# A two-block mixer and transformer kernel: weight rows stored as even and odd halves, and every weight product reading the two halves in turn

## The chip, the cores and the metric

The kernel runs on one core of one Trainium2 chip. The metric is the time of one execution on the device in microseconds. Three runs of the kernel before are given, and one execution of it was taken with the hardware profiler.

## What is computed

Two layers in a row on 256 tokens of width 2048, all in float32. The first block has an mLSTM and an HGRN2 branch behind one input projection, the second a spatial gating unit, stick-breaking attention and a gated feed-forward part. Both end with a gate on a small second input. Cut to the products with weight matrices, which the change touches:

```
def first_block(x, p, ...):
    proj = rmsnorm(x, norm_w) @ w_in                 # 2048 x 8200
    ...
    h = x + y @ w_out                                # 2048 x 2048
    e = p @ w_pe                                     # 256 x 2048
    h = h + sigmoid(rmsnorm(h, pe_norm_w) @ w_pg) * e
    return rmsnorm(h, final_norm_w)

def second_block(x, p, ...):
    proj = rmsnorm_2(x, attn_norm_g) @ w_in          # 2048 x 9216
    ...
    merged = sigmoid(g_a) * (y_a @ w_up_a) + sigmoid(g_b) * (y_b @ w_up_b)
    x = x + merged @ w_o
    hid = rmsnorm_2(x, ffn_norm_g) @ w_ffn_in        # 2048 x 11264
    x = x + (silu(gate) * up) @ w_ffn_out            # 5632 x 2048
    ple = p @ w_ple
    return x + sigmoid(rmsnorm_2(x, ple_norm_g) @ w_ple_gate) * ple
```

## The kernel before

Tokens lie on the output partitions: a product has 128 tokens as its stationary operand (a 128x128 block of the transposed activations) and a row of 512 weight columns, on 128 partitions, as its moving operand. The 256 tokens are T = 2 such blocks. An output slab is 512 columns (COLS) wide and takes two PSUM banks (`acc2(n)`, one for each token block). A piece is two blocks of 128 weight rows (PK = 2) of one slab, 128 x 2 x 512 numbers.

Float32 products are made of three products in the type float32r. The weights are split into a high part `whi` and a low part `wlo`, the activations into `act[0]` and `act[1]`; high times high, low times high and high times low are added. So a standard piece (the function `piece`, L1342 and L1347) issues 2 blocks x 2 token blocks x 3 = 12 products of 128x512. There are 512 of these pieces. For part of the second block's large matrices a seven-product scheme (M1 to M7) is used in place of eight half-size ones. Its pieces (`s_piece`, L1699 and L1703) treat one block of 128 tokens, or a sum of two, and so issue 6 products each. There are 336 of them. `first_piece` (L1370 to L1381) and `last_piece` (L1358) are the first and the last standard piece with finer waits.

A piece travels so. The SP queue loads weights from DRAM in pairs of pieces into `raw`, a ring of 8 places. ScalarE copies a place to `whi` (L915, for the seven-product scheme L1164), which rounds it to float32r. VectorE writes `wlo` as `raw` minus `whi` (L1851, L2507). Both `whi` and `wlo` are rings of 4 (RING). PE waits for `hi_ready` before the products with `whi` and for `lo_ready` before those with `wlo`, and gives the place back by `piece_used`, for which ScalarE waits before it writes the place again:

```
                act.activation(whi[:, g % RING], raw_piece(g), ACT.Copy).then_inc(hi_ready, 1)
                dve.tensor_tensor(wlo[:, g % RING], raw_piece(g), whi[:, g % RING].bitcast(F32), ALU.subtract)\
                    .then_inc(lo_ready, 1)
```

The weight blocks that the seven-product scheme needs as sums are made element by element, by transfers that add in DRAM (`summed`) and by VectorE.

Between the pieces, at fixed places of PE's program, stand the other matmuls: transposes through the identity, the recurrent branches, attention scores (L1589, L1590, moving `qT`, plain float32) and the spatial mixing (L1627). The last takes as its moving operand `vs[:, :, g * P:(g + 1) * P]`, 2 x 128 columns, that is two runs of 128 neighbours.

The order of the work is written out by hand on each engine, the seven-product part by the class `Plan`. The change alters none of it. The host function `_lay_out` brings the weights into the order in which the transfers read them. Before the change, the 512 columns of a slab lie in each weight row as they come.

In the profile's names of a matmul the output stands left of the arrow, and right of it the moving operand and then the stationary one.

Of the kernel before, what the change touches and what calls it, by code (L numbers as in the profile page):

```python
# [36 lines left out]
P = 128  # L37
# [4 lines left out]
COLS = 512  # L42
PK = 2

RAW = 8
RING = 4
# [265 lines left out]
def two_blocks_kernel(nc, A, out):  # L312
# [4 lines left out]
    with ctx:  # L317
# [20 lines left out]
        whi = sb("whi", [P, RING, PK, COLS], F32R)  # L338
        wlo = sb("wlo", [P, RING, PK, COLS], F32R)
# [9 lines left out]
        actA = [sb(f"actA_{x}", [P, KD, S], F32R, at=ra) for x in ("hi", "lo")]  # L349
# [141 lines left out]
        def aux_taken(eng, u, i=0):  # L491

            eng.wait_ge(aux_free[u % 4], u // 4 + 1 + i)
# [140 lines left out]
        def acc2(n):  # L634
            return acc[:, 2 * (n % 2):2 * (n % 2) + 2, :]
# [673 lines left out]
        def _(pe):  # L1309
# [19 lines left out]
            def free(u):  # L1329
                if u >= 4:  # L1330
                    aux_taken(pe, u - 4)

            def piece(n, p, act, k, last, i=0, slabs=0):

                g = SLABS[n][p]
                if p == 0 and n >= 2:
                    slab_taken(pe, n - 2, i * (slabs // 2))
                pe.wait_ge(hi_ready, g + 1 + i * ROUND)
                for c in range(PK):
                    for t in range(T):  # L1340
                        for x in range(2):
                            pe.matmul(acc2(n)[:, t, :], act[x][:, k + c, t * P:(t + 1) * P], whi[:, g % RING, c, :],  # L1342
                                      start=(p == 0 and c == 0 and x == 0), stop=False)
                pe.wait_ge(lo_ready, g + 1 + i * ROUND)
                for c in range(PK):
                    for t in range(T):
                        ins = pe.matmul(acc2(n)[:, t, :], act[0][:, k + c, t * P:(t + 1) * P], wlo[:, g % RING, c, :],  # L1347
                                        start=False, stop=(last and c == PK - 1))
                ins.then_inc(piece_used, 1)

            def last_piece(n, p, act, k):

                g = SLABS[n][p]
                pe.wait_ge(lo_ready, g + 1)
                for t in range(T):
                    for c in range(PK):
                        for x, w in ((0, whi), (1, whi), (0, wlo)):
                            ins = pe.matmul(acc2(n)[:, t, :], act[x][:, k + c, t * P:(t + 1) * P], w[:, g % RING, c, :],  # L1358
                                            start=False, stop=(c == PK - 1 and w is wlo))
                    ins.then_inc(sem("last_tile"), 1)  # L1360

# [3 lines left out]
            def first_piece():  # L1365

                pe.wait_ge(sem("x_hi"), 1)
                pe.wait_ge(sem("first_half_hi"), 1)
                for t in range(T):
                    pe.matmul(acc2(0)[:, t, :], actA[0][:, 0, t * P:(t + 1) * P], whi[:, 0, 0, :], start=True, stop=False)  # L1370
                pe.wait_ge(sem("x_lo"), 1)
                for t in range(T):
                    pe.matmul(acc2(0)[:, t, :], actA[1][:, 0, t * P:(t + 1) * P], whi[:, 0, 0, :], start=False, stop=False)
                pe.wait_ge(hi_ready, 1)
                for t in range(T):
                    for x in range(2):
                        pe.matmul(acc2(0)[:, t, :], actA[x][:, 1, t * P:(t + 1) * P], whi[:, 0, 1, :], start=False, stop=False)
                pe.wait_ge(lo_ready, 1)
                for c in range(PK):
                    for t in range(T):  # L1380
                        ins = pe.matmul(acc2(0)[:, t, :], actA[0][:, c, t * P:(t + 1) * P], wlo[:, 0, c, :], start=False, stop=False)  # L1381
                ins.then_inc(piece_used, 1)

            def warm(n):
# [115 lines left out]
            for s in range(16):  # L1500
                n = FIRST["A"] + s
                for p in range(8):
                    w = s * 8 + p
# [39 lines left out]
            for s in range(4):  # L1543
                n = FIRST["C"] + s
                for p in range(8):
                    k = (KD // 2 + p * PK) % KD
# [19 lines left out]
            for s in range(4):  # L1566
                n = FIRST["D"] + s
# [63 lines left out]
            for s in range(10):  # L1631
                n = FIRST["E1"] + s
                for p in range(8):
# [3 lines left out]
                    w = s * 8 + p  # L1637
# [21 lines left out]
            def s_piece(g, c, m, q):  # L1659

                if m == "M1" and q == 0:
                    if c == 0:
                        for i in range(4):
                            aux_taken(pe, AUX[("ybT", i)])
                    else:
                        pe.wait_ge(sem("s_second_row"), c)
                    if c == M_GROUPS:
                        for i in range(4, 8):
                            aux_taken(pe, AUX[("hH", i)])
                    if c > M_GROUPS:  # L1670
                        pe.wait_ge(sem("tr_taken"), fills_before(g, "e"))
                if m == "M2" and q == 0 and c > 0:
                    pe.wait_ge(sem("hid_odd_ready"), c)
                    pe.wait_ge(sem("tr_taken"), fills_before(g, "a"))
                if m == "M7" and q == 0:
                    pe.wait_ge(sem("merge_forms_lo" if c < M_GROUPS else "forms_lo"), 4)
                if m == "M5" and q == 0 and c > 0:
                    pe.wait_ge(sem("s_first_row"), c)
                if m == "M6" and q == 0:
                    pe.wait_ge(sem("s_first"), c + 1)  # L1680
                if m == "M3" and q == 0:
                    pe.wait_ge(sem("s_fifth"), c + 1)
                o = s_bank(c, m)
                if m == "M7" and q == 0 and c >= M_GROUPS:
                    pe.wait_ge(sem("tr_taken"), fills_before(g, "d"))
                if m == "M4" and q == 0:
                    pe.wait_ge(sem("s_sixth"), c + 1)
                whole, parts = (actB, merge_form_T) if c < M_GROUPS else (actA, formT)

                def lhs(x, k):  # L1690
                    if m in S_FORM:
                        return parts[x][:, S_FORM[m], k, :]
                    return whole[x][:, KD // 2 + k, P:S] if m == "M4" else whole[x][:, k if m == "M1" else KD // 2 + k, 0:P]

                onto = m in ("M6", "M3")
                pe.wait_ge(hi_ready, g + 1)
                for k in range(PK):
                    for x in range(2):
                        pe.matmul(o, lhs(x, q * PK + k), whi[:, g % RING, k, :], start=(q == 0 and k == 0 and x == 0 and not onto),  # L1699
                                  stop=False, skip_group_check=onto)  # L1700
                pe.wait_ge(lo_ready, g + 1)
                for k in range(PK):
                    ins = pe.matmul(o, lhs(0, q * PK + k), wlo[:, g % RING, k, :], start=False, stop=(q == 3 and k == PK - 1),  # L1703
                                    skip_group_check=onto)
                ins.then_inc(piece_used, 1)

# [7 lines left out]
            for kind, g, *x in PLAN.merge:  # L1714
                if kind == "s":
                    s_piece(g, x[0], x[2], x[3])
                else:
                    n, role, j, q, p = x
# [6 lines left out]
                t = g - PLAN.g_plan  # L1725
# [15 lines left out]
            for s in range(4):  # L1741
                n = FIRST["G"] + s
# [52 lines left out]
            for kind, g, *x in PLAN.ffn:  # L1795
                if kind == "s":
                    s_piece(g, x[0], x[2], x[3])
                else:
                    n, role, j, q, p = x
# [955 lines left out]

def _lay_out(inputs, np):

    def blocks(w):
        k, n = w.shape
        return w.reshape(k // 512, 4, P, n // COLS, COLS).transpose(3, 0, 2, 1, 4)  # L2760

    def short(w):
        return w.reshape(PK, P, w.shape[1] // COLS, COLS).transpose(1, 2, 0, 3)

    laid = {name: inputs[name] for name in _AS_THEY_ARE}
    x = inputs["x"][0]
    laid["x"] = x.reshape(T, P, D).transpose(1, 0, 2)
    columns = x.T.reshape(KD, P, S).transpose(1, 0, 2).reshape(P, KD * S)
    laid["x_gain_and_columns"] = np.concatenate([inputs["norm_w"].reshape(KD, P).T, columns], axis=1)
    for name in _WEIGHTS:  # L2770
        laid[name] = blocks(inputs[name][0])
    w = inputs["w_in"][0]
    laid["w_in"] = blocks(np.concatenate([w[:, :MI], w[:, HQ:]], axis=1))
    laid["w_in_gates"] = w[:, MI:HQ].reshape(KD, P, HQ - MI).transpose(1, 0, 2)
    for name in ("w_pe", "w_ple_2"):
        laid[name] = short(inputs[name][0])
    for name in ("p", "p_2"):
        laid[name] = inputs[name][0, 0].T.reshape(PK, P, S).transpose(1, 0, 2)
    laid["w_s_2"] = inputs["w_s_2"][0].transpose(2, 0, 1)
    laid["vectors"] = np.concatenate([inputs[name].reshape(-1, P) for name in _VECTORS], axis=0).T  # L2780
    return {name: np.ascontiguousarray(a) for name, a in laid.items()}
# [16 lines left out]
```

## Time and profile before

| | before |
|---|---|
| median of 3 runs | 1984.99 us |
| lowest, highest | 1984.66, 1985.69 us |
| profiled execution: span from the first to the last instruction | 1982.4 us |
| PE busy | 1973.1 us (100%) |
| load of stationary operands (PEld) busy | 1642.8 us (83%) |
| VectorE (DVE) busy | 1476.6 us (74%) |
| ScalarE (ACT) busy | 1147.5 us (58%) |
| GpSimd (POOL) busy | 114.5 us (6%) |
| moved by DMA | 535.95 MB, 270 GB/s in the mean |

The page gives no other time for the profiled execution than its span, so the span stands for it here. Busy time is the time in which at least one instruction of the engine was under way. Matmuls overlap, and the end of one is modelled, so the pace of PE is read from the starts of the instructions and not from their lengths. The granted clock is the share of full speed that TensorE's clock had.

### The profile page before, as it was taken

The page shows a single profiled execution, that of the slowest core. Times are in us where ns is not written, and L with a number is a line of the kernel's source. Part 1 is how long each engine was busy: PE and PEld are TensorE (multiplying, and loading weights), DVE is VectorE, ACT ScalarE, POOL GpSimd, SP SyncE. Part 2 cuts the span into 40 slices and gives each one's busy share as a digit, 9 for nine tenths or more (in the row PEclk, how much of TensorE's full clock was granted, in tenths as well). Part 3 has the DMA queues.
Part 4 walks back from the last instruction along what each step waited for, and adds up shares of the span by engine and source line. Part 5 has one row for each costly group of instructions (what it writes and reads, how often), then busy time and mean ns, then how long its engine had stood idle before and what let it go on. Part 6 is the DMA issues. An engine that isn't in the chain of part 4 may idle for free.

```text
span 1982.4 us, 23547 instructions
## 1 busy us (share of the span) xinstructions
PE 1973.1 (100%) x9126; PEld 1642.8 (83%) x9126; DVE 1476.6 (74%) x1571; ACT 1147.5 (58%) x1417; POOL 114.5 (6%) x140
## 2 busy tenths in 40 slices
PE   9999999999999999999999999999999999999999
PEld 7888888888888888888888888888888888888887
DVE  6877776555666666768888657888988898888764
ACT  7546444554466455556666445666666666666553
POOL 1000010000001110000000000000000000000000
PEclk9999999999999999999999999999999999999999
DMA  9788798999889999858797876788878887877553
GB/s 377 255 250 278 234 322 275 323 327 313 278 287 298 342 341 299 255 195 253 283 299 244 313 242 238 236 299 278 273 229 303 271 264 240 308 251 235 209 178 125
DMA packets 86816, 535.95 MB, mean 270 GB/s; under 512 B 10417, under 2 KB 11185, under 8 KB 40753
## 3 DMA queue, kind: packets, MB, share of 16 engines
q1 hardware_dynamic: 72736, 458.69, 60.9%
q0 software_dynamic: 13824, 75.50, 20.0%
q8 instruction: 72, 1.18, 0.2%
q10 hardware_dynamic: 144, 0.26, 0.0%
q14 instruction: 40, 0.32, 0.0%
HBM read 529.69 MB, written 105.38 MB: 320 GB/s over the span
## 4 chain that ended last, share of the span: by engine, by line
PE 96%; DVE 2%; DMA 1%; ACT 1%; issue 0%; SPq 0%; DVEq 0%; ACTq 0%
PE acc L1342 45%; PE acc L1347 22%; PE aux L1699 15%; PE aux L1703 8%; PE aux L1325 1%; PE aux L1415 1%; DMA raw<-in_w_in 1%; DVE wlo L1851 1%; PE aux L1780 0%; DVE wlo L2507 0%; ACT whi L915 0%; PE aux L1405 0%; PE aux L1430 0%; DVE att_z L2353 0%; PE aux L1316 0%
## 5 line engine op out<-in xcount | busy, mean ns | idle before, releaser
L1851 DVE TENSOR_TENSOR wlo<-raw,whi 128x1024 fp32r<-128x1024 f32 x512 | 624.2, 1225 | 359.7 <-ACT whi L915 350.2
L915 ACT ACTIVATE whi<-raw 128x1024 fp32r<-128x1024 f32 x511 | 537.3, 1058 | 535.0 <-PE acc L1347 490.0
L1342 PE MATMUL acc<-whi,actA_hi 128*128 128x512 f32 x892 | 351.6, 394 | 0.0
L1342 PE MATMUL acc<-whi,actA_lo 128*128 128x512 f32 x892 | 347.4, 390 | 0.0
L1342 PE MATMUL acc<-whi,actB_hi 128*128 128x512 f32 x796 | 312.7, 393 | 0.2 <-DVE actB_lo L2624 0.2
L1342 PE MATMUL acc<-whi,actB_lo 128*128 128x512 f32 x796 | 309.9, 389 | 0.0
L1164 ACT ACTIVATE whi<-ple 128x1024 fp32r<-128x1024 f32 x192 | 202.3, 1060 | 136.0 <-PE acc L1347 87.4
L2507 DVE TENSOR_TENSOR wlo<-ple,whi 128x1024 fp32r<-128x1024 f32 x192 | 231.9, 1223 | 37.6 <-ACT whi L1164 30.6
L1347 PE MATMUL acc<-wlo,actA_hi 128*128 128x512 f32 x892 | 238.7, 389 | 0.0
L1347 PE MATMUL acc<-wlo,actB_hi 128*128 128x512 f32 x796 | 213.2, 390 | 1.2 <-DVE wlo L1851 1.2
L2507 DVE TENSOR_TENSOR wlo<-raw,whi 128x1024 fp32r<-128x1024 f32 x144 | 175.4, 1223 | 36.1 <-ACT whi L1164 30.9
L1347 PEld LDWEIGHTS acc<-wlo,actA_hi 128*128 128x128 f32 x892 | 167.5, 188 | 35.1
L1342 PEld LDWEIGHTS acc<-whi,actA_hi 128*128 128x128 f32 x892 | 167.6, 188 | 34.2 <-issue 0.3
L1164 ACT ACTIVATE whi<-raw 128x1024 fp32r<-128x1024 f32 x144 | 152.6, 1060 | 73.9 <-PE acc L1347 48.9
L1342 PEld LDWEIGHTS acc<-whi,actA_lo 128*128 128x128 f32 x892 | 167.6, 188 | 33.5
L1347 PEld LDWEIGHTS acc<-wlo,actB_hi 128*128 128x128 f32 x796 | 149.3, 188 | 33.0 <-DVE wlo L1851 2.0
L1342 PEld LDWEIGHTS acc<-whi,actB_hi 128*128 128x128 f32 x796 | 149.5, 188 | 31.0 <-DVE actB_lo L2624 0.9
L1342 PEld LDWEIGHTS acc<-whi,actB_lo 128*128 128x128 f32 x796 | 149.6, 188 | 30.1
L1699 PE MATMUL aux<-whi,actB_hi 128*128 128x512 f32 x360 | 140.4, 390 | 0.0
L1699 PE MATMUL aux<-whi,actB_lo 128*128 128x512 f32 x360 | 140.1, 389 | 0.0
L1703 PE MATMUL aux<-wlo,actB_hi 128*128 128x512 f32 x360 | 111.0, 389 | 0.3 <-DVE wlo L2507 0.3
L1699 PE MATMUL aux<-whi,actA_hi 128*128 128x512 f32 x216 | 85.1, 394 | 0.0
(360 smaller groups left out, 2391.9 us busy)
## 6 DMA issues: line engine op xcount, KB each, us to landing
raw<-in_w_in SPq DMA_DIRECT2D x108, 1024.0 KB, 7.6
raw<-in_w_ffn_out SPq DMA_DIRECT2D x44, 1024.0 KB, 7.0
summed<-in_w_ffn_in POOLq DMA_DIRECT2D x36, 1024.0 KB, 11.9
raw<-in_w_ffn_in SPq DMA_DIRECT2D x72, 512.0 KB, 7.5
ple<-summed SPq DMA_DIRECT2D x24, 1024.0 KB, 4.8
raw<-summed SPq DMA_DIRECT2D x48, 512.0 KB, 4.8
ple<-in_w_ffn_in SPq DMA_DIRECT2D x18, 1024.0 KB, 7.6
ple<-in_w_ffn_in POOLq DMA_DIRECT2D x36, 512.0 KB, 9.8
```

Of the source, the lines that this page charges most:

```text
L915: act.activation(whi[:, g % RING], raw_piece(g), ACT.Copy).then_inc(hi_ready, 1)
L1164: act.activation(whi[:, g % RING], s_source(c, m, q), ACT.Copy).then_inc(hi_ready, 1)
L1325: ins = pe.transpose(bank(u)[:, c * S + t * P:c * S + (t + 1) * P], src[:, t, (c0 + c) * P:(c0 + c + 1) * P], ident[:, :])
L1342: pe.matmul(acc2(n)[:, t, :], act[x][:, k + c, t * P:(t + 1) * P], whi[:, g % RING, c, :], start=(p == 0 and c == 0 and x == 0), stop=False)
L1347: ins = pe.matmul(acc2(n)[:, t, :], act[0][:, k + c, t * P:(t + 1) * P], wlo[:, g % RING, c, :], start=False, stop=(last and c == PK - 1))
L1415: ins = pe.matmul(bank(u)[:, j * m:(j + 1) * m], Kp[n % 2][:, c:c + P], Qp[n % 2][:, j * m:(j + 1) * m], start=True, stop=True)
L1699: pe.matmul(o, lhs(x, q * PK + k), whi[:, g % RING, k, :], start=(q == 0 and k == 0 and x == 0 and not onto), stop=False, skip_group_check ...
L1703: ins = pe.matmul(o, lhs(0, q * PK + k), wlo[:, g % RING, k, :], start=False, stop=(q == 3 and k == PK - 1), skip_group_check=onto)
L1851: dve.tensor_tensor(wlo[:, g % RING], raw_piece(g), whi[:, g % RING].bitcast(F32), ALU.subtract)\
L2507: dve.tensor_tensor(wlo[:, g % RING], s_source(c, m, q), whi[:, g % RING].bitcast(F32), ALU.subtract)\
```

## The change

On the host, in each row of 512 columns of every weight matrix the even columns come first and then the odd ones (`woven` in `_lay_out`). `w_in_gates`, the 8 gate columns, and the small arrays stay as they are. On PE, the moving operand of every weight product is no longer the row of 512 as it lies, but a pattern of 256 x 2 elements over it: element 0 of the first half, element 0 of the second half, element 1 of the first half, and so on (`woven` beside `piece`). So column j of the output is again column j of the weights. The pattern's inner step is 256 elements (1024 bytes), its outer step one element.

All products keep their shape, number and order; every engine's and every queue's instructions stand in the order of before. Buffers, waits and the stationary operands are unchanged.

```
+            def woven(ring, g, c):
+                return ring[:, g % RING, c, :].rearrange("p (h j) -> p j h", h=2)
...
             def piece(n, p, act, k, last, i=0, slabs=0):
...
-                            pe.matmul(acc2(n)[:, t, :], act[x][:, k + c, t * P:(t + 1) * P], whi[:, g % RING, c, :],
+                            pe.matmul(acc2(n)[:, t, :], act[x][:, k + c, t * P:(t + 1) * P], woven(whi, g, c),
...
-                        ins = pe.matmul(acc2(n)[:, t, :], act[0][:, k + c, t * P:(t + 1) * P], wlo[:, g % RING, c, :],
+                        ins = pe.matmul(acc2(n)[:, t, :], act[0][:, k + c, t * P:(t + 1) * P], woven(wlo, g, c),
...
-                        pe.matmul(o, lhs(x, q * PK + k), whi[:, g % RING, k, :], start=(q == 0 and k == 0 and x == 0 and not onto),
+                        pe.matmul(o, lhs(x, q * PK + k), woven(whi, g, k), start=(q == 0 and k == 0 and x == 0 and not onto),
...
-                    ins = pe.matmul(o, lhs(0, q * PK + k), wlo[:, g % RING, k, :], start=False, stop=(q == 3 and k == PK - 1),
+                    ins = pe.matmul(o, lhs(0, q * PK + k), woven(wlo, g, k), start=False, stop=(q == 3 and k == PK - 1),
...
 def _lay_out(inputs, np):
+    def woven(w):
+        k, n = w.shape
+        return w.reshape(k, n // COLS, COLS // 2, 2).swapaxes(2, 3).reshape(k, n)
...
     def blocks(w):
         k, n = w.shape
-        return w.reshape(k // 512, 4, P, n // COLS, COLS).transpose(3, 0, 2, 1, 4)
+        return woven(w).reshape(k // 512, 4, P, n // COLS, COLS).transpose(3, 0, 2, 1, 4)
     def short(w):
-        return w.reshape(PK, P, w.shape[1] // COLS, COLS).transpose(1, 2, 0, 3)
+        return woven(w).reshape(PK, P, w.shape[1] // COLS, COLS).transpose(1, 2, 0, 3)
```

`first_piece` and `last_piece` are edited in the same way.

## Rows read from the trace of the kernel before

**Rows 1.** Page, busy time of each engine; granted clock in tenths, 40 slices.
```profile
PE 1973.1 (100%) x9126; PEld 1642.8 (83%) x9126; DVE 1476.6 (74%) x1571; ACT 1147.5 (58%) x1417; POOL 114.5 (6%) x140
...
PEclk9999999999999999999999999999999999999999
```

**Rows 2.** Page, the chain that ended last, by engine and by line.
```profile
PE 96%; DVE 2%; DMA 1%; ACT 1%; issue 0%; SPq 0%; DVEq 0%; ACTq 0%
PE acc L1342 45%; PE acc L1347 22%; PE aux L1699 15%; PE aux L1703 8%; PE aux L1325 1%; PE aux L1415 1%; DMA raw<-in_w_in 1%; DVE wlo L1851 1%; PE aux L1780 0%; DVE wlo L2507 0%; ACT whi L915 0%; PE aux L1405 0%; PE aux L1430 0%; DVE att_z L2353 0%; PE aux L1316 0%
```

**Rows 3.** Windows, whole span, PE of lines L1342, L1347, L1699, L1703 in turn.
```profile
0.00:1983.00 1983.00, 1016.93 (x4080) 1.00 0.81 270
...
0.00:1983.00 1983.00, 546.16 (x2040) 1.00 0.81 270
...
0.00:1983.00 1983.00, 360.79 (x1344) 1.00 0.81 270
...
0.00:1983.00 1983.00, 207.07 (x672) 1.00 0.81 270
```

**Rows 4.** Timeline of PE, two pieces (start us, us, line, shapes, count).
```profile
703.31 0.39 PE L1342 MATMUL acc<-whi,actB_hi 128*128 128x512 f32 x1
703.54 0.39 PE L1342 MATMUL acc<-whi,actB_lo 128*128 128x512 f32 x1
...
705.13 1.07 PE L1347 MATMUL acc<-wlo,actB_hi 128*128 128x512 f32 x4
706.03 0.39 PE L1342 MATMUL acc<-whi,actB_hi 128*128 128x512 f32 x1
```

**Rows 5.** Timeline of PE, one short piece and the next.
```profile
1000.11 0.39 PE L1699 MATMUL aux<-whi,merge_form_hi 128*128 128x512 f32 x1
...
1001.47 0.39 PE L1699 MATMUL aux<-whi,merge_form_hi 128*128 128x512 f32 x1
```

**Rows 6.** Timeline of the loads of the stationary operand (PEld).
```profile
706.04 0.19 PEld L1342 LDWEIGHTS acc<-whi,actB_lo 128*128 128x128 f32 x1
706.26 0.19 PEld L1342 LDWEIGHTS acc<-whi,actB_hi 128*128 128x128 f32 x1
```

**Rows 7.** Timeline of PE, attention scores in plain fp32.
```profile
708.75 0.59 PE L1589 MATMUL aux<-qT,kT 128*128 128x256 f32 x2
709.18 0.38 PE L1590 MATMUL aux<-qT,kT 128*128 128x128 f32 x2
709.40 0.60 PE L1589 MATMUL aux<-qT,kT 128*128 128x256 f32 x2
709.84 0.38 PE L1590 MATMUL aux<-qT,kT 128*128 128x128 f32 x2
710.06 0.60 PE L1589 MATMUL aux<-qT,kT 128*128 128x256 f32 x2
710.49 0.38 PE L1590 MATMUL aux<-qT,kT 128*128 128x128 f32 x2
```

**Rows 8.** Timeline of PE, spatial mixing and the next piece.
```profile
832.58 1.89 PE L1627 MATMUL aux<-sgu_v,wsT 128*128 128x256 f32 x8
834.12 0.58 PE L1342 MATMUL acc<-whi,actB_hi 128*128 128x512 f32 x1
```

**Rows 9.** Page, costliest groups on VectorE and ScalarE (idle before, releaser last).
```profile
L1851 DVE TENSOR_TENSOR wlo<-raw,whi 128x1024 fp32r<-128x1024 f32 x512 | 624.2, 1225 | 359.7 <-ACT whi L915 350.2
L915 ACT ACTIVATE whi<-raw 128x1024 fp32r<-128x1024 f32 x511 | 537.3, 1058 | 535.0 <-PE acc L1347 490.0
```

**Rows 10.** Timeline, the first and the last weight products and the end.
```profile
6.79 0.70 PE L1370 MATMUL acc<-whi,actA_hi 128*128 128x512 f32 x2 [0.96 <-ACT whi L979]
...
1977.22 0.39 PE L1358 MATMUL acc<-wlo,actB_hi 128*128 128x512 f32 x1
...
1979.70 0.42 DVE L2747 TENSOR_TENSOR resid<-resid,gate 128x256 f32<-128x256 f32 x1
```

More of the change, by code:

```diff
@@ L1357, in last_piece @@
                         for x, w in ((0, whi), (1, whi), (0, wlo)):
-                            ins = pe.matmul(acc2(n)[:, t, :], act[x][:, k + c, t * P:(t + 1) * P], w[:, g % RING, c, :],
+                            ins = pe.matmul(acc2(n)[:, t, :], act[x][:, k + c, t * P:(t + 1) * P], woven(w, g, c),
                                             start=False, stop=(c == PK - 1 and w is wlo))
@@ L1369, in first_piece @@
                 for t in range(T):
-                    pe.matmul(acc2(0)[:, t, :], actA[0][:, 0, t * P:(t + 1) * P], whi[:, 0, 0, :], start=True, stop=False)
+                    pe.matmul(acc2(0)[:, t, :], actA[0][:, 0, t * P:(t + 1) * P], woven(whi, 0, 0), start=True, stop=False)
                 pe.wait_ge(sem("x_lo"), 1)
                 for t in range(T):
-                    pe.matmul(acc2(0)[:, t, :], actA[1][:, 0, t * P:(t + 1) * P], whi[:, 0, 0, :], start=False, stop=False)
+                    pe.matmul(acc2(0)[:, t, :], actA[1][:, 0, t * P:(t + 1) * P], woven(whi, 0, 0), start=False, stop=False)
                 pe.wait_ge(hi_ready, 1)
@@ L1376, in first_piece @@
                     for x in range(2):
-                        pe.matmul(acc2(0)[:, t, :], actA[x][:, 1, t * P:(t + 1) * P], whi[:, 0, 1, :], start=False, stop=False)
+                        pe.matmul(acc2(0)[:, t, :], actA[x][:, 1, t * P:(t + 1) * P], woven(whi, 0, 1), start=False, stop=False)
                 pe.wait_ge(lo_ready, 1)
@@ L1380, in first_piece @@
                     for t in range(T):
-                        ins = pe.matmul(acc2(0)[:, t, :], actA[0][:, c, t * P:(t + 1) * P], wlo[:, 0, c, :], start=False, stop=False)
+                        ins = pe.matmul(acc2(0)[:, t, :], actA[0][:, c, t * P:(t + 1) * P], woven(wlo, 0, c), start=False, stop=False)
                 ins.then_inc(piece_used, 1)
```

## The prediction

> **What bounds the kernel now.** I read the page's busy times first [rows 1]. TensorE (PE) is busy 1973.1 of 1982.4 us and the granted clock stands in its top tenth in every slice, that is at the 2.4 GHz level; VectorE has 74% and ScalarE 58%. The chain that ended last is the second view [rows 2]: 96% of it is PE, and the four weight-product lines L1342, L1347, L1699 and L1703 alone hold 45 + 22 + 15 + 8 = 90%. So nearly every microsecond of the span is a weight product, and what the products wait for hardly matters: PE is idle for 1982.4 - 1973.1 = 9.3 us in all.
>
> How many are they? The busy time by line has a count in brackets [rows 3]: 4080 + 2040 + 1344 + 672 = 8136, and the first and the last piece of the program, which have lines of their own, hold 12 each: 8160. All of them have the same shape, 128x512, and all of them are touched by the change.
>
> What does one cost? Not the 390 ns that a row gives as its length: those lengths overlap. The distance between starts counts. In the timeline an ordinary piece of 12 products starts at 703.31 and the next one at 706.03 [rows 4]: 2.72 us, or 0.2267 us a product. The short pieces of L1699 and L1703 go at the same pace: 6 products from 1000.11 to 1001.47 [rows 5], again 0.2267 us. 8160 x 0.2267 = 1850 us; the remaining 133 us of the span are the other matmuls and the idle time. At 2.4 GHz 512 columns take 0.2133 us, so the columns are streamed at one per clock, with 13 ns a product on top. The load of the stationary operand takes 0.19 us and starts as the product before it starts [rows 6]: it is hidden under the stream, but by little.
>
> **The change, part by part.** It moves, adds and removes no instruction on any engine, and the transfers have the same shapes and sizes. Three things are left to cost.
>
> 1. The host lays the weights out in another order inside each row of 512. The transfer of a piece, ScalarE's copy to the high part (1.06 us), VectorE's subtraction for the low part (1.23 us) and the sums of weight blocks go element by element over the same contiguous rows, so they cost what they did. Price 0. Their cover also stays: ScalarE waited 490 us for PE to give a ring slot back, VectorE 350 us for ScalarE [rows 9]. A slower PE makes these waits longer, a PE of the same speed leaves them.
>
> 2. The output of each product is written to PSUM in the order of before, column after column, and so is everything read from there. Price 0.
>
> 3. Each weight product now reads its moving operand in another order: element 0 of the row, element 256, element 1, element 257, and so on, a hop of 1 KB one way or the other after every element, where before it read 512 neighbours. Everything hangs on the price of that. No matmul of this trace has such an operand. The nearest on the cheap side is the spatial mixing, whose moving operand is two runs of 128 neighbours [rows 8]: four 256-column products and the step to the next piece take 1.54 us, 0.385 us each, against 0.43 us for a 256-column product of contiguous operands [rows 7]. One hop in the middle costs nothing; that bounds the price from below at 0, and I see no way in which the new order could gain. On the dear side stand the plain fp32 products [rows 7]: each product appears as two records, and L1589, with 2 x 256 columns, takes 0.43, 0.44 and 0.43 us until L1590 starts, 0.433 us for 512 columns streamed. At the same granted clock that is one column every two clocks, the 1.2 GHz pace. So TensorE has a half-pace stream in this very kernel. Counted by product, not by record, that is 0.433 us for 256 columns, so 0.866 us for 512: the upper bound, four clocks a column.
>
> Between 0.2267 and 0.866 us I take 0.433. The reason is an assumption that no row shows, that at one column per clock the columns come in twos or fours from one access; where neighbours no longer come one after the other, the natural next step is one column an access at the half pace, which the trace shows the engine to run at. The sum: 8160 x (0.433 - 0.2267) = +1683 us on the span of 1982.4 us, so 3666 us. The page gives no time of the profiled execution but this span; the median of the runs, 1984.99 us, is 2.6 us above it, and with that I arrive at **3668 us**. The beginning (the first weights arrive before the first product at 6.79 us) and the end (about 5 us of gate, addition and store after the last product [rows 10]) don't change.
>
> The Trainium skill speaks against this change: SBUF — State Buffer, section "Door 1: The DMA port swizzle", says that SBUF has 16-byte lines, that accesses run at full rate only with at least two hits on a line one after the other, and that each step to another line pays. By that rule every column here pays, since neighbours in the stream are 1 KB apart; it gives no figure for TensorE. With the half pace the sum would be the one above, and without the rule it would be 1985 us. No row of this trace shows such a step, so it neither agrees nor disagrees.
>
> **The rivals.** *Not slower: both halves stay at hand.* The stream is two ascending streams in turn, and each comes back to its own neighbourhood after one element. If the read side keeps the last piece fetched for each of the two, or fetches ahead by the access pattern, it fetches as much as before and the pace stays one column a clock. Place: the moving read of all 8160 products; price 0; it decides as soon as two columns from two places are had within 0.4533 us / 512 = 0.89 ns. Time 1985 us. For it: the two-run operand is free [rows 8], and the stationary load streams from another tile at the same time as the moving operand without a loss of pace [rows 4, 6]. Against it: both of these have long runs in each stream, and the second comes through a read of its own kind. That the pattern doesn't reach the engine as written ends at the same time and is counted here. The Trainium skill has a case for this rival: Vector Engine (DVE) Microarchitecture Reference, section 5.2, reports that a single read stream alternating between two regions every element ran at the full rate, on VectorE; no row here shows it on any engine.
>
> *Four clocks a column.* If each column needs a whole fetch of its own and this takes as long as it takes to fetch four neighbours, a product costs 0.866 us: +8160 x 0.639 = +5217 us, 7202 us. For it: the full pace over contiguous elements may rest on fours. Against it: no single record of the trace streams as slowly; the plain products get there only by two records [rows 7]. The same section of the Trainium skill gives 1.73 ns a column for VectorE with a source that hops every element, against 1.054 ns contiguous; 512 columns at 1.73 ns are an estimate of 0.886 us from that page, 7365 us in the end, near this rival.
>
> *In between.* Only some of the hops cost, say every second pair of columns twice its time: pitch about 0.33 us, +8160 x 0.103 = 2826 us. Nothing in the trace speaks for a particular value.
>
> *The clock.* If PE, standing still for every second clock, were granted 1.2 GHz, the products would hardly change (512 columns at 1.2 GHz are 0.427 us), but the other matmuls, 133 us less 9.3 us idle, would double: +123 us, 3791 us. This only widens the forecast.
>
> **How the numbers follow.** Half pace: 0.45. Its own range goes from 0.427 us a product (3617 us) over the 13 ns a product of today on top of 0.433 (0.446 us, 3775 us) to the clock case (3791 us): 3610 to 3800. Not slower: 0.27. Faster: 0.01, with no mechanism to name. In between: 0.08. Four clocks or another price beyond the half pace: 0.19. The range must reach over the not-slower case and the half pace to hold 8 in 10: 1980 to 3800 us holds 0.27 + 0.08 + 0.45 = 0.80 and leaves out the four clocks. A measurement of this kernel can tell about 0.2% (4 us) from no change. Faster by more than that 0.01, within it 0.27, slower 0.72.
>
> **What would show it.** If right, the distance from piece to piece of L1342 in the timeline is 5.2 us for 12 products and 2.6 us for 6 (before: 2.72 and 1.36), PE stays 99 to 100% busy, the granted clock stays at the top, the L1589 pairs keep 0.43 us, and ScalarE's wait for PE grows by some 1700 us while DVE and ACT are busy for as long as before. The forecast is wrong if the piece distance stays 2.72 us (the halves stay at hand), if it is near 10.4 us (four clocks), or if ScalarE, VectorE or a transfer turns up in the chain of waits, which none of my cases has.

## The result, and the profile after

| | before | after |
|---|---|---|
| median | 1984.92 us (4 runs, 1984.66 to 1985.69) | 1905.14 us (4 runs, 1903.34 to 1907.28) |
| ratio of the times | | 0.9598, 95% interval 0.9584 to 0.9611 |
| span of the profiled execution | 1982.4 us | 1905.5 us |

The change makes the kernel 4% faster. I had forecast 3668 us, in a range from 1980 to 3800, and had given "faster" a chance of 0.01.

The page of the changed kernel, its busy times, the granted clock in tenths over 40 slices, and the chain that ended last (they answer to [rows 1, 2]; L1346, L1351, L1703 and L1707 are the lines of the weight products now):

```profile
PE 1888.7 (99%) x9126; PEld 1654.2 (87%) x9126; DVE 1473.2 (77%) x1571; ACT 1141.7 (60%) x1417; POOL 118.9 (6%) x140
...
PEclk9999999999999999999999999999999999999999
...
PE 88%; DVE 5%; DMA 3%; issue 2%; ACT 2%; POOL 0%; SPq 0%; ACTq 0%; DVEq 0%; POOLq 0%
PE acc L1346 42%; PE acc L1351 21%; PE aux L1703 13%; PE aux L1707 6%; DVE wlo L2511 2%; PE aux L1325 2%; PE aux L1419 1%; DMA raw<-in_w_in 1%; DMA ple<-in_w_ffn_in 1%; DVE wlo L1855 1%; ACT whi L915 1%; DVE ple L2506 1%; DMA ple<-in_w_in 1%; PE aux L1784 0%; ACT whi L1164 0%
```

PE is still the bound, a little less closely. It is idle for 16.8 us (1905.5 - 1888.7) against 9.3, and its share of the chain falls from 96 to 88%. The busy time of the four weight-product lines over the whole span, in the order L1346, L1351, L1703, L1707 (as [rows 3]: stretch, its length, busy time of PE and count, clock, DMA):

```profile
0.00:1906.00 1906.00, 971.75 (x4080) 1.00 0.84 281
...
0.00:1906.00 1906.00, 524.65 (x2040) 1.00 0.84 281
...
0.00:1906.00 1906.00, 346.48 (x1344) 1.00 0.84 281
...
0.00:1906.00 1906.00, 200.50 (x672) 1.00 0.84 281
```

The counts are those of before, and the busy times are lower by 45.2, 21.5, 14.3 and 6.6 us, 87.6 us in all. The timeline of PE shows it product by product (start, length, line; as [rows 4]):

```profile
704.81 0.38 PE L1346 MATMUL acc<-whi,actB_hi 128*128 128x512 f32 x1
705.03 0.38 PE L1346 MATMUL acc<-whi,actB_lo 128*128 128x512 f32 x1
...
706.54 1.03 PE L1351 MATMUL acc<-wlo,actB_hi 128*128 128x512 f32 x4
707.40 0.38 PE L1346 MATMUL acc<-whi,actB_hi 128*128 128x512 f32 x1
```

A piece of 12 products takes 707.40 - 704.81 = 2.59 us, where it took 2.72: 0.2158 us a product instead of 0.2267. All the starts of the trace give a median distance of 216 ns against 227. So 8160 x 10.9 ns = 89 us should have gone, and 76.9 us of span did (79.8 us by the medians; the profiled execution is the longest of the four). Part of the missing 12 us is in two stops. The total wait of PE for VectorE (who waited for whom, total in us, times, longest):

```profile
PE acc L1351 <- DVE wlo L1855: 5.4, 2, 3.7
```

One stop is 3.7 us long, the other 1.7. The longer stands behind the attention logarithms of VectorE: the part of the weights that PE waits for (`wlo`) is made only after L2357, the third operation of these logarithms. The timeline of PE around it, and then that of VectorE before it:

```profile
708.91 0.38 PE L1346 MATMUL acc<-whi,actB_lo 128*128 128x512 f32 x1
713.00 2.08 PE L1351 MATMUL acc<-wlo,actB_hi 128*128 128x512 f32 x4 [3.71 <-DVE wlo L1855]
714.87 1.06 PE L1603 MATMUL aux<-att_l,later 128*128 128x256 f32 x2
...
709.93 1.75 DVE L2357 SCALAR_TENSOR_TENSOR att_z<-att_z,att_ab 128x1536 f32<-128x1536 f32 x1
711.72 2.36 DVE L1855 TENSOR_TENSOR wlo<-raw,whi 128x1024 fp32r<-128x1024 f32 x2
```

and the same stretch in windows of 4 us, with two finer ones behind them (length, busy time of PE and count, granted clock, DMA):

```profile
708.00:712.00 4.00, 1.29 (x6) 1.00 0.81 346
712.00:716.00 4.00, 3.00 (x8) 0.54 0.52 154
716.00:720.00 4.00, 4.00 (x18) 0.61 1.03 246
...
712.00:713.00 1.00, 0.00 (x1) 0.65 0.00 0
713.00:719.00 6.00, 6.00 (x18) 0.50 0.90 239
```

PE stopped for 3.7 us. In the last microsecond of the stop the granted clock was 0.65 in the mean, and in the six after it 0.50, the 1.2 GHz level. An estimate of what this cost is half of the six microseconds, 3 us. With the 7.5 us of added idle time that is 10.5 of the 12 us. Before, PE waited 0.6 us at this place, and the clock was 1.00 in the windows around it.

The work of VectorE and ScalarE did not change (as [rows 9]):

```profile
L1855 DVE TENSOR_TENSOR wlo<-raw,whi 128x1024 fp32r<-128x1024 f32 x512 | 624.0, 1226 | 318.2 <-ACT whi L915 310.5
L915 ACT ACTIVATE whi<-raw 128x1024 fp32r<-128x1024 f32 x511 | 534.2, 1054 | 482.5 <-PE acc L1351 439.4
```

### The profile page after: what moved, and what is told of

Read it like the earlier page. It is cut to its first block, busy times and chain, and to the rows that moved or that the text cites. A ratio compares the mean times of both kernels' runs of the same rounds, so it can differ in the third digit from the quotient of the medians.

```text
span 1905.5 us, 23547 instructions
## 1 busy us (share of the span) xinstructions
PE 1888.7 (99%) x9126; PEld 1654.2 (87%) x9126; DVE 1473.2 (77%) x1571; ACT 1141.7 (60%) x1417; POOL 118.9 (6%) x140
## 4 chain that ended last, share of the span: by engine, by line
PE 88%; DVE 5%; DMA 3%; issue 2%; ACT 2%; POOL 0%; SPq 0%; ACTq 0%; DVEq 0%; POOLq 0%
PE acc L1346 42%; PE acc L1351 21%; PE aux L1703 13%; PE aux L1707 6%; DVE wlo L2511 2%; PE aux L1325 2%; PE aux L1419 1%; DMA raw<-in_w_in 1%; DMA ple<-in_w_ffn_in 1%; DVE wlo L1855 1%; ACT whi L915 1%; DVE ple L2506 1%; DMA ple<-in_w_in 1%; PE aux L1784 0%; ACT whi L1164 0%
## 5 line engine op out<-in xcount | busy, mean ns | idle before, releaser
L1346 PE MATMUL acc<-whi,actA_hi 128*128 128x512 f32 x892 | 342.3, 384 | 0.2 <-ACT whi L915 0.2
L1346 PE MATMUL acc<-whi,actA_lo 128*128 128x512 f32 x892 | 338.1, 379 | 0.0
L1346 PE MATMUL acc<-whi,actB_hi 128*128 128x512 f32 x796 | 304.6, 383 | 1.7 <-ACT whi L915 1.5
L1346 PE MATMUL acc<-whi,actB_lo 128*128 128x512 f32 x796 | 301.7, 379 | 0.0
L1351 PE MATMUL acc<-wlo,actA_hi 128*128 128x512 f32 x892 | 228.9, 379 | 0.0
L1351 PE MATMUL acc<-wlo,actB_hi 128*128 128x512 f32 x796 | 205.4, 381 | 5.4 <-DVE wlo L1855 5.4
L1346 PEld LDWEIGHTS acc<-whi,actA_hi 128*128 128x128 f32 x892 | 168.7, 189 | 24.4 <-issue 1.5
L1351 PEld LDWEIGHTS acc<-wlo,actA_hi 128*128 128x128 f32 x892 | 168.6, 189 | 23.9
L1346 PEld LDWEIGHTS acc<-whi,actA_lo 128*128 128x128 f32 x892 | 168.7, 189 | 22.7
L1351 PEld LDWEIGHTS acc<-wlo,actB_hi 128*128 128x128 f32 x796 | 150.8, 190 | 27.6 <-DVE wlo L1855 6.2
L1346 PEld LDWEIGHTS acc<-whi,actB_hi 128*128 128x128 f32 x796 | 150.5, 189 | 23.9 <-ACT whi L915 2.3
L1346 PEld LDWEIGHTS acc<-whi,actB_lo 128*128 128x128 f32 x796 | 150.5, 189 | 20.6
L1703 PE MATMUL aux<-whi,actB_hi 128*128 128x512 f32 x360 | 136.9, 380 | 0.3 <-ACT whi L1164 0.3
L1703 PE MATMUL aux<-whi,actB_lo 128*128 128x512 f32 x360 | 136.4, 379 | 0.0
L1707 PE MATMUL aux<-wlo,actB_hi 128*128 128x512 f32 x360 | 107.3, 380 | 0.8 <-DVE wlo L2511 0.7
L1703 PE MATMUL aux<-whi,actA_hi 128*128 128x512 f32 x216 | 83.0, 384 | 0.0
```

The lines of the kernel that those rows point to most:

```text
L1703: pe.matmul(o, lhs(x, q * PK + k), woven(whi, g, k), start=(q == 0 and k == 0 and x == 0 and not onto), stop=False, skip_group_check=onto)
L1707: ins = pe.matmul(o, lhs(0, q * PK + k), woven(wlo, g, k), start=False, stop=(q == 3 and k == PK - 1), skip_group_check=onto)
```

## The experiments

**The order of reading or the layout?** The first run leaves the host's layout as it was, and changes only the operand; the second does the reverse. Both permute the columns of the output.

```
 e1:  return woven(w).reshape(...)              ->  return w.reshape(...)
 e2:  ring[:, g % RING, c, :].rearrange(...)    ->  ring[:, g % RING, c, :]
```

> The changed kernel with the host's layout of before: the weight products read element 0, element 256, element 1 and so on, but the rows hold their columns as they come (so the columns of the output come out permuted). The theory that the read order alone makes the products faster expects the time of the changed kernel, 1905 us within 4, a piece distance of 2.59 us and a ratio to before of 0.960. The rival that the new layout helps (transfers, ScalarE's or VectorE's work on the rows) expects 1985 us and 2.72 us.

> The changed kernel with the host's new layout, but every weight product reads its row of 512 in order as before (so the columns of the output come out permuted). The theory of the read order expects the time of before, 1985 us within 4, piece distance 2.72 us. The rival of the layout expects 1905 us.

Measured: the read order alone 1904.72 us, ratio 0.9598 (0.9584 to 0.9612). The layout alone 1985.62 us, ratio 1.0004 (0.9994 to 1.0013). Two neighbouring piece starts in the timeline of each, the read order alone first:

```profile
704.76 0.38 PE L1346 MATMUL acc<-whi,actB_hi 128*128 128x512 f32 x1
...
707.35 0.38 PE L1346 MATMUL acc<-whi,actB_hi 128*128 128x512 f32 x1
```

```profile
700.85 0.39 PE L1346 MATMUL acc<-whi,actB_hi 128*128 128x512 f32 x1
...
703.57 0.39 PE L1346 MATMUL acc<-whi,actB_hi 128*128 128x512 f32 x1
```

2.59 us and 2.72 us, both as the theory of the read order had them. The whole gain is in the order in which the moving operand is read. Transfers and the two splitting engines have no part in it.

**Which orders are fast?** One kernel holds sixteen orders, each on its own source line, so that each can be read by its line:

```
+            OF = [lambda o, s, w, c, **k: pe.matmul(o, s, w[:, c, :], **k),
+                  lambda o, s, w, c, **k: pe.matmul(o, s, w[:, c, :].rearrange("p (h j) -> p j h", h=2), **k),
...
-                            pe.matmul(acc2(n)[:, t, :], act[x][:, k + c, t * P:(t + 1) * P], whi[:, g % RING, c, :],
+                            OF[g % 16](acc2(n)[:, t, :], act[x][:, k + c, t * P:(t + 1) * P], whi[:, g % RING], c,
```

> The kernel before, in which the standard pieces take one of sixteen read orders of the moving row, by piece number modulo 16; the seven-product pieces stay contiguous (columns of the output come out permuted). Read is the distance of products per order; contiguous has 0.2267 us and two halves in turn 0.2158 us. Theory A, neighbours fetched one after the other are what is slow, and any order in which successive columns come from different places is fast: 2, 4, 8 or more places in turn 0.216, runs of 2 neighbours 0.216, runs of 8 or 16 neighbours and two runs of 256 0.227. Theory B, the pattern's form counts, not the places (any operand that isn't one plain run is fast): all orders but the contiguous one 0.216, two runs of 256 too. Theory C, two streams in turn are a special case that is kept at hand, while many places in turn cost a fetch for every column, as in my prediction: 2 in turn 0.216, but with 8 or more in turn 0.43 us or more, and the order with a step of 4 or 8 elements too.

Measured, the median distance of starts of 512-column products (330 to 385 of each order):

| order of the 512 columns | ns |
|---|---|
| contiguous; two runs of 256 from two rows | 227; 227 |
| 2 places in turn, 1 KB apart; 2 KB apart | 216; 216 |
| 4 places in turn | 275 |
| 8 places | 487 |
| 16; 32; 64 places (the last a step of 32 bytes) | 433; 433; 431 |
| 128 places (a step of 16 bytes) | 460 |
| 256 places (a step of 8 bytes: even columns, then odd) | 452 |
| 2 places in turn, runs of 2; 4; 8; 16 columns | 340; 254; 245; 240 |
| 4 places in turn, runs of 2 columns | 443 |

The first product of pieces in the timeline (contiguous had L1334): two places L1335, two runs L1336, runs of two L1337, runs of four L1338, four places L1339, eight L1340, sixteen L1341:

```profile
788.61 0.38 PE L1335 MATMUL acc<-whi,actA_hi 128*128 128x512 f32 x1
...
791.20 0.40 PE L1336 MATMUL acc<-whi,actA_hi 128*128 128x512 f32 x1
...
793.95 0.50 PE L1337 MATMUL acc<-whi,actA_hi 128*128 128x512 f32 x1
...
798.01 0.42 PE L1338 MATMUL acc<-whi,actA_hi 128*128 128x512 f32 x1
...
801.02 0.44 PE L1339 MATMUL acc<-whi,actA_hi 128*128 128x512 f32 x1
...
804.30 0.72 PE L1340 MATMUL acc<-whi,actA_hi 128*128 128x512 f32 x1
...
810.22 0.61 PE L1341 MATMUL acc<-whi,actA_hi 128*128 128x512 f32 x1
```

From start to start of the rows that follow each other directly: 2.59 us for L1335, 2.75 for L1336, 4.06 for L1337, 3.01 for L1338, 3.28 for L1339, and 5.92 for L1340. Theory A falls (runs of two columns from two places are dear, not fast), and so does B (two runs of 256 stay at 227). Theory C holds in its core: two places are a case of their own. From 16 to 64 places the price is 431 to 433 ns, the half pace that I had forecast for two places, and with 128 and 256 places 460 and 452. Its bound "0.43 us or more" holds for 8 places too. What none of the three had: four places cost only 275 ns, and the price does not rise evenly with their number.

**By the column, by the product, by the load?** Sizes and types vary here, and what the smaller products leave out is not computed:

```
+                  lambda o, s, w, c, **k: pe.matmul(o[:, 0:256], s, w[:, c, 0:256], **k),
+                  lambda o, s, w, c, **k: pe.matmul(o[0:32, 0:256], s[:, 0:32], w[:, c, 0:256], **k),
...
+                  lambda o, s, w, c, **k: pe.matmul(o, s.bitcast(mybir.dt.bfloat16)[:, 1:256:2], w[:, c, :].bitcast(mybir.dt.bfloat16)[:, 1:1024:2], **k),
```

> The kernel before, in which most products of the standard pieces are smaller or of another type, by piece number modulo 16: 512, 384 or 256 columns, contiguous or with two halves in turn, with a stationary operand of 128 or of 32 columns; and two orders in which the high halves of the numbers are read as bfloat16 (the rest of the product is left out, the outputs are not the reference's). If contiguous reading costs by the column, the extra over the other order is 11 ns at 512, 8 at 384 and 5.5 at 256 columns. If it is a fixed cost of a product, it is 11 ns at all three. If it comes from the load of the stationary operand under the stream, it is gone or smaller with 32 columns of it (a shorter load). In bfloat16, 512 columns out of the same 2 KB in order: 0.227 us if the time goes by bytes passed over in the row, 0.216 us if by bytes read.

Measured, median distance in ns, contiguous and two halves in turn, and the contiguous one less the columns' own time at 2.4 GHz:

| columns | 128 stationary columns | 32 stationary columns | contiguous less own time |
|---|---|---|---|
| 512 | 227, 216 | 231, 216 | 14, 18 |
| 384 | 174, 162 | 174, 162 | 14, 14 |
| 256 | 120, 112 | 117, 109 | 13, 10 |

Three starts each of 256 columns with 32 stationary ones, contiguous (L1344) and in turn (L1345), and two of bfloat16 with a step of 4 bytes (L1346):

```profile
503.85 0.28 PE L1344 MATMUL acc<-whi,actB_hi 128*32 128x256 f32 x1
503.96 0.28 PE L1344 MATMUL acc<-whi,actB_lo 128*32 128x256 f32 x1
504.08 0.28 PE L1344 MATMUL acc<-whi,actB_hi 128*32 128x256 f32 x1
...
505.24 0.27 PE L1345 MATMUL acc<-whi,actB_hi 128*32 128x256 f32 x1
505.35 0.27 PE L1345 MATMUL acc<-whi,actB_lo 128*32 128x256 f32 x1
505.46 0.27 PE L1345 MATMUL acc<-whi,actB_hi 128*32 128x256 f32 x1
...
507.02 0.39 PE L1346 MATMUL acc<-whi,actB_lo 128*128 128x512 bf16 x1
507.25 0.39 PE L1346 MATMUL acc<-whi,actB_hi 128*128 128x512 bf16 x1
```

With 128 stationary columns the contiguous product has 13 to 14 ns over its columns' time at all three lengths, as a fixed amount of the product would. With 32 it has 18, 14 and 10 ns, which falls with the columns. So this run does not decide between the two. It does decide on the length of the load. With 32 stationary columns the load takes 108 ns (median of its rows) instead of 188, and the loss doesn't go away; at 512 columns it is larger. A cost that any load would bring, whatever its length, isn't excluded. The many places don't hang on the load either: 64 and 128 places with 32 stationary columns take 430 and 460 ns, as with 128. The order in turn has 2 to 3 ns over, except for 256 columns under a load of 128 (5 ns). The bfloat16 product, which passes over the same 2 KB in order but reads half the bytes, takes 225 ns: the loss is there as well. One row was not expected by any theory: the same bfloat16 product with two halves in turn takes 541 ns. So what two places give was seen for float32r columns, and this one form of bfloat16, 2 bytes out of every 4, loses by them. Why, and whether bfloat16 columns that lie side by side would, no run tells.

**How far apart must the two places be?** Seven of the sixteen kinds are two places in turn within blocks of columns; these two give 16 and 8 bytes:

```
+                  lambda o, s, w, c, **k: pe.matmul(o, s, w[:, c, :].rearrange("p (a h j) -> p a j h", a=64, h=2), **k),
+                  lambda o, s, w, c, **k: pe.matmul(o, s, w[:, c, :].rearrange("p (a h j) -> p a j h", a=128, h=2), **k),
```

> The kernel before, in which the standard pieces take other read orders or operands by piece number modulo 16, the first product of a slab and the last ones staying whole (columns permuted or a few left out, so the outputs are not the reference's). Two places in turn at a distance of 512, 256, 128, 64, 32, 16 and 8 bytes; contiguous with 508 columns from column 0 and from column 4 and 510 from column 1; two places at 1020 and 960 bytes; six places; four places at 256 bytes; a stationary operand with a step of 2; and pieces in which contiguous and two-in-turn products alternate. Theory A, contiguous products lose a fixed 11 ns at their start, whatever the stationary operand and the alignment are, and two places in turn avoid it: 0.216 us for two places at every distance, 11 ns more than the columns' own time and 2.5 ns for all contiguous ones. Theory B, what counts is in which part of the memory the two places lie: 0.216 us only at some distances (1 and 2 KB among them), and near distances such as 16 or 8 bytes, or 1020 and 960 bytes, give another time, up to 0.34 us or more. In the alternating pieces the loss shows after the contiguous product if it belongs to its end, and after the other if it belongs to the start of the next contiguous one.

Measured: 216 ns at 512, 256, 128, 64, 32 and 16 bytes, and 227 at 8 bytes. 510 columns at 1020 bytes 215 and 480 columns at 960 bytes 202, again 2 ns over the columns' time. Contiguous: 508 columns 227 from column 0 and from column 4, 510 columns from column 1 235; a stationary operand of 64 columns with a step of 2 228. Six places (504 columns) 291, four places at 256 bytes 283. First products of pieces at 16 bytes (L1339), at 8 bytes (L1340), and the next kind (L1341):

```profile
522.06 0.38 PE L1339 MATMUL acc<-whi,actA_hi 128*128 128x512 f32 x1
...
524.65 0.39 PE L1340 MATMUL acc<-whi,actA_hi 128*128 128x512 f32 x1
...
527.39 0.39 PE L1341 MATMUL acc<-whi,actA_hi 128*128 128x508 f32 x1
```

2.59 and 2.74 us. So for this operand two places in turn were fast at every distance tried from 16 bytes on, and a swap inside 16 bytes (0, 2, 1, 3) gave nothing; the edge lies between 8 and 16 bytes, and nothing between was tried. Theory A fails at 8 bytes, and its fixed 11 ns at column 1, where 510 contiguous columns have 22.5 ns over their own time. Theory B was right that near distances have an edge, but no distance was dearer than contiguous.

The Trainium skill, SBUF — State Buffer, section "Door 1: The DMA port swizzle", has 16-byte lines in SBUF, with full rate only where at least two accesses one after the other fall on a line. The edge between 8 and 16 bytes agrees with that size. The rule itself doesn't hold for two places: every column changes the line, and 216 ns is the fastest order of all, while runs of two columns from two places keep two on a line and took 340 ns. From 8 places on, no order of single columns came under 430 ns, and there the rule fits.

The pieces in which contiguous (L1348) and in-turn products (L1365) alternate:

```profile
502.44 0.40 PE L1348 MATMUL acc<-whi,actB_hi 128*128 128x512 f32 x1
502.67 0.38 PE L1365 MATMUL acc<-whi,actB_lo 128*128 128x512 f32 x1
502.89 0.39 PE L1348 MATMUL acc<-whi,actB_hi 128*128 128x512 f32 x1
503.12 0.38 PE L1365 MATMUL acc<-whi,actB_lo 128*128 128x512 f32 x1
```

After a contiguous product the next one starts 232 ns later, after an in-turn product 215 ns later (medians; the rows show 0.23 and 0.22). The loss stays with the contiguous product, whatever follows.

**Was the sum sound?** The changed kernel with sixteen places in place of two, laid out to match:

```
-                return ring[:, g % RING, c, :].rearrange("p (h j) -> p j h", h=2)
+                return ring[:, g % RING, c, :].rearrange("p (h j) -> p j h", h=16)
...
-        return w.reshape(k, n // COLS, COLS // 2, 2).swapaxes(2, 3).reshape(k, n)
+        return w.reshape(k, n // COLS, COLS // 16, 16).swapaxes(2, 3).reshape(k, n)
```

> The changed kernel with sixteen places in turn instead of two, the rows laid out to match. In the sixteen orders a product with 16 places took 0.433 us, the price that my prediction had for two places. If the sum of the prediction was sound but for that price, the time is 1905 + 8160 x (0.433 - 0.216) = 3676 us, within 20 us. If something else than the products' pace (other engines, the transfers) had a part, it is off by more.

Measured: 3677.14 us (2 runs), ratio 1.852 (1.8486 to 1.8554). Attention scores and weight products in its timeline:

```profile
1400.82 0.61 PE L1593 MATMUL aux<-qT,kT 128*128 128x256 f32 x2
1401.27 0.38 PE L1594 MATMUL aux<-qT,kT 128*128 128x128 f32 x2
...
1403.86 0.62 PE L1346 MATMUL acc<-whi,actB_lo 128*128 128x512 f32 x1
1404.29 0.62 PE L1346 MATMUL acc<-whi,actB_hi 128*128 128x512 f32 x1
```

Here nearly my forecast of 3668 us stands as a measurement, of another order. The plain fp32 product takes 0.45 us (0.43 to 0.44 before) and the mean granted clock is 0.999: count and cover were read rightly. That the sum met the time within 1 us is in part luck. The products took 435 ns here (median of the starts), not 433, which makes 3692 us. Against that PE was idle for 7.3 us (3675.6 - 3668.3) instead of 16.8, and the 3 us of low clock behind the stop were gone: 3680 us.

The clock fell in this run too, and without a stop of PE: in the mean of the window from 514 to 520 us it was 0.50, right behind 2 us of small products with operands on 4 partitions (L1471, L1478). The products of sixteen places kept their 0.43 us in that window. In the kernel before, no fall stands behind the same small products.

**The missing 12 us.** The changed kernel with one operation of VectorE (L2357 above) a piece later:

```
                 strict_blocks(Lp).then_inc(sem("att_l"), 1)
+            def att_logs_z(b):
                 link(dve.scalar_tensor_tensor(out=zt[:, :, :], in0=zt[:, :, :], scalar=0.0, in1=ab[:, :, :], op0=ALU.min,
...
+                        if w == z0 + 10:
+                            att_logs_z(b)
```

> The changed kernel, in which VectorE does the third operation of the attention logarithms one piece later, so that the split of a piece's low part comes before it. In the changed kernel PE waited 3.9 and 1.9 us for VectorE at these two places. If the part of the expected gain that did not come (8160 x 10.9 ns = 89 us against 77 us of span) lies in such waits, this gives back 2 to 5 us: 1900 to 1903 us. If the waits are only passed on to the next one, 1905 us.

Measured: 1899.38 us (5 runs, 1897.68 to 1900.24), ratio 0.9564 (0.9551 to 0.9577) where the changed kernel had 0.9598: 5.8 us less by the medians, a little more than the 2 to 5 us expected. With the last run below, which ties with it, it is the fastest version of the study. The windows of the stop, as above:

```profile
708.00:712.00 4.00, 2.08 (x10) 1.00 0.98 397
712.00:716.00 4.00, 4.00 (x28) 1.00 0.92 287
716.00:720.00 4.00, 4.00 (x20) 1.00 0.99 188
```

PE still waits 1.9 us (busy 2.08 of 4), but the clock stays at 1.00. The other stop, of 1.7 us, is gone. In the profiled executions the span fell by 1905.5 - 1898.5 = 7.0 us: 1.8 and 1.7 us of waiting and some 3 us of low clock make 6.5 of them. That the long stop made the clock fall is argued from this one stop: in the profiled executions before, after and of this run, it is the only one behind which the clock fell.

> The kernel before with the logarithms apart alone, all products contiguous. If the waits that this edit takes away were made by the faster products, it does little here, where PE waited 0.8 us at each of the two places: 1983 to 1985 us. If the edit is worth its 5.7 us by itself: 1979 us.

Measured on the kernel before: 1983.17 us, ratio 0.9989 (0.998 to 0.9999), some 2 us, where the two waits were 0.6 us each. So the larger part of those 5.8 us were a wait that the faster products had made, and the clock that followed it.

> The kernel of the logarithms apart, in which two places in turn lie 16 bytes apart (within blocks of 8 columns: 0, 4, 1, 5, 2, 6, 3, 7) and the rows are laid out to match, instead of two halves 1 KB apart. In the distances 16 bytes gave 0.216 us a product and 8 bytes 0.227 us. If that holds for the whole kernel: 1899 us, within 4 of the kernel of the logarithms apart. If the short distance costs anything outside the standard pieces, it is above 1903 us.

Measured: 1899.47 us, ratio 0.9568 (0.9554 to 0.9583). In the whole kernel, 16 bytes do as well as 1 KB.

## Why the prediction was wrong

- **The bound, the count and the cover: right.** 8160 products, PE as the bound, no change in the work of VectorE, ScalarE or the queues: the layout alone gives 1.0004, and the sixteen places, where the price is 0.433 to 0.435, come out at 3677 us where my sum with 0.433 said 3668.
- **The price of the read order: the step that failed.** I wrote that between 0.2267 and 0.866 us I take 0.433, because the columns come in twos or fours from one access and a hop breaks that up. The price is 0.216. For two places the assumption is wrong; for 16 to 64 it gives the number measured, which doesn't show that the reason given for it is the right one. I took a property of many places for one of every hop.
- **"That bounds the price from below at 0, and I see no way in which the new order could gain": the worse mistake.** The rows had the room for a gain in them: 0.2267 us a product against 0.2133 us for its columns, 13.4 ns that I read as belonging to the product "on top" and never asked about. 8160 x 13.4 ns = 109 us was the most that any change to the products' pace could give; the change gave 89 us of them. And the rows held contiguous products with less on top: the plain fp32 ones [rows 7] start 8 records with 1536 columns in 710.06 - 708.75 = 1.31 us, where two clocks a column make 1.28, so some 4 ns a record. The range ended at 1980 us, at a place where no row stood.
- **The spatial mixing: misread.** I gave it 0.385 us a product, by the step to the next piece [rows 8]. But that piece's first product starts while the mixing is still under way, and its second comes only at 834.54 (the row below this list). From 832.58 to 834.54 are 1.96 us; less one product of 0.227 that leaves 0.43 us for each of the four, the same as contiguous. So a hop in the middle is indeed free, and these rows were no hint of a gain; two runs of 256 give 227 ns as well.
- **The rival "both halves stay at hand": nearest to the result.** Two ascending streams in turn do keep the full pace, as its words had it, and its price 0 was too high by 10.9 ns a product. That something is kept at hand for each of them, no run shows. A chance of 0.27 was too little. The Trainium skill, Vector Engine (DVE) Microarchitecture Reference, section 5.2, reports a single read stream alternating between two regions at the full rate, on VectorE. The runs show the full pace for TensorE as well, with float32r columns.
- **Four clocks a column:** no order of 4-byte columns came near 0.866 us; the dearest was 0.487.
- **The clock:** it fell, but not over the run, as my rival had it: in the changed kernel behind a stop of 3.7 us and for some 7 us only. With products of sixteen places the mean stayed at 0.999.
- **"If ScalarE, VectorE or a transfer turns up in the chain of waits, which none of my cases has":** they did, with 10% of the chain (5 + 3 + 2) instead of 4%.

The second product behind the spatial mixing, in the timeline of PE before:

```profile
834.54 0.40 PE L1342 MATMUL acc<-whi,actB_lo 128*128 128x512 f32 x1
```

What stays open is why a contiguous product has 13 to 14 ns over its columns' time and an in-turn one 2 to 3. Shown is that most of it is gone with two places from 16 bytes on, that it stays with the contiguous product whatever follows, and that neither the length of the stationary operand's load nor the layout of the row makes it. Whether it is a fixed amount or goes by the column, and its cause, are not shown.

## What to carry to other kernels

Compare a product's pace with its columns' own time at the granted clock; where the difference is not zero, it is a term that a change may win back, and a bound for "no gain" needs a row that excludes it. On a PE-bound kernel with float32r products of 512 columns, reading the moving row as two places in turn, 16 bytes or more apart, gave 10.9 ns a product; four places, runs of a few columns from two places, and the one bfloat16 form in two halves all cost. Once the bound engine is faster by 5%, look for the waits that come up behind it and for the clock after them: here one operation moved by one piece gave back 5.8 us.

## What I had not expected of the hardware

- Two places in turn are faster than contiguous reading, 216 against 227 ns for 512 float32r columns.
- The price of many places is not even: 275 (4), 291 (6, with 504 columns), 487 (8), 433 (16) ns; and runs of two columns from two places, 340 ns, are dearer than single columns from the same two.
- Contiguous columns from column 1 on: 235 ns for 510, where 508 from column 0 or 4 take 227.
- bfloat16 columns with a step of 4 bytes take 225 ns in order and 541 ns with two halves in turn.
- Behind a stop of PE of 3.7 us the granted clock was 0.50 for six microseconds; behind the shorter stops of 1.7 us, and of 1.9 us at the same place, it was not. In the run with sixteen places it was 0.50 as well behind 2 us of products with operands on 4 partitions, with PE busy.
